# Opening of a three-sub-layer decoder kernel: twelve of its 24 weight units multiplied in fp32 from the landed weights, without high and low parts

## The reference, cut to what matters

```
cond = silu(c)
mod = cond @ ada_w[l] + ada_b[l]                 # 2048 x 18432 weights
sh1, sc1, gt1, sh2, sc2, gt2, sh3, sc3, gt3 = split(mod, 9)
h = rms_norm(x, g_pre) * (1 + sc1) + sh1
gate, up = split(h @ ffn1_w_in, 2)               # 2048 x 11008 weights
y = (silu(gate) * up) @ ffn1_w_out
x = x + 0.5 * gt1 * rms_norm(y, g_post)
... token mixer with sh2, sc2, gt2; second SwiGLU with sh3, sc3, gt3
```

## Time and profile before

| | us |
|---|---|
| median of 3 runs (1950.99 to 1953.15) | 1952.62 |
| the profiled execution's own time | 1952.52 |
| its span, first to last instruction | 1950.7 |
| TensorE busy | 1899.6 (97%) |
| VectorE busy | 1394.3 (71%) |
| ScalarE busy | 846.6 (43%) |
| the opening (to the first group of 8 units) | about 150 |

### The profile page before, as it was taken

The page is one execution under the profiler, slowest core; times in us unless marked ns, Lnnn a source line. Parts: engine busy times, 40 slices in busy tenths (PEclk is TensorE's granted clock), DMA queues, the critical chain, the costliest instruction groups (busy, mean ns, idle before and its releaser), DMA issues.

```text
span 1950.7 us, 21974 instructions
## 1 busy us (share of the span) xinstructions
PE 1899.6 (97%) x8875; PEld 1568.6 (80%) x8875; DVE 1394.3 (71%) x1403; ACT 846.6 (43%) x1075; POOL 79.3 (4%) x137
## 2 busy tenths in 40 slices
PE   5999999999999999899999998999999999999997
PEld 5888888888888889687777786888888888888895
DVE  5979889888888989766775477666665665455565
ACT  4244443444444334564555434644344434443443
POOL 0001000000000000000000010000000000000000
PEclk9999999999999999999999999999999999999999
DMA  9999999999999999564434443766667655556551
GB/s 367 371 354 361 360 339 333 350 346 345 339 342 353 372 322 340 166 191 139 130 110 137 148 151 121 244 239 237 236 230 249 234 194 194 191 186 215 170 199 76
DMA packets 208677, 486.85 MB, mean 250 GB/s; under 512 B 8560, under 2 KB 29760, under 8 KB 193472
## 3 DMA queue, kind: packets, MB, share of 16 engines
q1 hardware_dynamic: 191920, 365.81, 54.3%
q0 software_dynamic: 16224, 117.47, 16.4%
q10 hardware_dynamic: 432, 2.16, 0.3%
HBM read 483.31 MB, written 2.10 MB: 249 GB/s over the span
## 4 chain that ended last, share of the span: by engine, by line
PE 91%; DVE 3%; DMA 2%; ACT 2%; issue 1%; SPq 0%; DVEq 0%; ACTq 0%
PE ps_g L1385 10%; PE ps_u L1385 10%; PE ps_g L1387 10%; PE ps_g L1386 10%; PE ps_u L1387 10%; PE ps_u L1386 10%; PE ps_t L1385 4%; PE ps_t L1387 4%; PE ps_t L1386 4%; PE ps_y L1387 4%; PE ps_y L1385 4%; PE ps_y L1386 4%; DMA ada_raw<-in_ada_w 2%; DVE arena L1131 1%; PE ps_t L1436 1%
## 5 line engine op out<-in xcount | busy, mean ns | idle before, releaser
L882 DVE TENSOR_TENSOR w_lo<-w_raw,w_hi 128x1024 fp32r<-128x1024 f32 (+2 forms) x608 | 724.6, 1200 | 472.6 <-ACT w_hi L544 471.3
L544 ACT ACTIVATE w_hi<-w_raw 128x1024 fp32r<-128x1024 f32 (+2 forms) x608 | 632.9, 1042 | 926.8 <-PE ps_u L1387 331.2
L1385 PE MATMUL ps_g<-w_hi,xT_hi 128*128 128x512 f32 (+1 forms) x880 | 346.1, 393 | 19.2 <-DVE xT_lo L1160 9.1
L1385 PE MATMUL ps_u<-w_hi,xT_hi 128*128 128x512 f32 (+2 forms) x880 | 344.3, 391 | 1.0 <-issue 0.8
L1387 PE MATMUL ps_g<-w_hi,xT_lo 128*128 128x512 f32 (+1 forms) x880 | 340.9, 387 | 0.0
L1386 PE MATMUL ps_g<-w_lo,xT_hi 128*128 128x512 f32 (+1 forms) x880 | 340.6, 387 | 0.0
L1387 PE MATMUL ps_u<-w_hi,xT_lo 128*128 128x512 f32 (+2 forms) x880 | 338.6, 385 | 0.0
L1386 PE MATMUL ps_u<-w_lo,xT_hi 128*128 128x512 f32 (+2 forms) x880 | 338.4, 385 | 0.0
L906 DVE SCALAR_TENSOR_TENSOR arena<-ada_raw,cond,arena 128x2048 f32<-128x2048 f32 x108 | 253.4, 2346 | 5.0 <-DMA ada_raw<-in_ada_w 5.0
L1385 PEld LDWEIGHTS ps_g<-w_hi,xT_hi 128*128 128x128 f32 x880 | 166.1, 189 | 59.2 <-issue 20.4
L1385 PEld LDWEIGHTS ps_u<-w_hi,xT_hi 128*128 128x128 f32 x880 | 165.2, 188 | 36.6 <-issue 6.0
(11 more groups left out here) (246 smaller groups left out, 1717.3 us busy)
## 6 DMA issues: line engine op xcount, KB each, us to landing
w_raw<-in_ffn_w_in SPq DMA_DIRECT2D x157, 1024.0 KB, 6.7
ada_raw<-in_ada_w POOLq DMA_DIRECT2D x112, 1024.0 KB, 6.7
w_raw<-in_ffn_w_out SPq DMA_DIRECT2D x80, 1024.0 KB, 6.7
w_raw<-in_mix_w_in SPq DMA_DIRECT2D x32, 1024.0 KB, 5.1
ada_raw<-in_ada_w SPq DMA_DIRECT2D x32, 512.0 KB, 8.8
arena<-in_ada_w SPq DMA_DIRECT2D x32, 512.0 KB, 9.8
w_raw<-in_mix_w_out SPq DMA_DIRECT2D x16, 1024.0 KB, 5.0
w_raw<-in_ffn_w_in SPq DMA_DIRECT2D x16, 768.0 KB, 5.8
```

The lines of the kernel that those rows point to most:

```text
L544: nc.scalar.activation(w_hi[:, u % 4, 0:n, 0:width], w_raw[:, s, 2 * hf:2 * hf + n, 0:width], ACT.Copy).then_inc(hi_done, 1)
L882: nc.vector.tensor_tensor(w_lo[:, u % 4, 0:n, 0:width], w_raw[:, s, 2 * hf:2 * hf + n, 0:width], w_hi[:, u % 4, 0:n, 0:width].bitcast(F32) ...
L1385: nc.tensor.matmul(o, a_hi[:, k, rows], w_hi[:, b, c, 0:width], start=start, stop=False)
```

## The change

In the three full strips, the units of blocks 0 and 1 (v mod 6 below 4: four of six, twelve in all) are no longer split. TensorE multiplies them in fp32, from the scaled input `xT_raw` and the landed weights `w_raw`: 4 matmuls in the place of 12. The two units of block 2, and all of the short strips, are split as before. What follows from it in the code: the part slots and the counts of `hi_done` and `lo_done` go over the split units alone; ScalarE and VectorE walk a strip's two split units only, with the input pairs and ada tiles set between them; a weight load that takes a raw slot last used by a raw unit waits for TensorE (`pe_used`) in place of VectorE (`lo_done`).

```
+RAW_BLOCKS = 2
+def first_split(v):
+    return v >= 2 * OPENING * FULL or v % (2 * OPENING) // 2 >= RAW_BLOCKS
+SPLIT_UNITS = [v for v in range(8 * OPENING) if first_split(v)]
+SPLIT_SLOT0 = -len(SPLIT_UNITS) % 4
...
 # SP, first_weights
-                need(sp, lo_done, 2 * (q - 4) + 2)
+                before = 2 * (q - 4) + 1
+                if before > 0 and first_split(before):
+                    sp.wait_ge(lo_done, split_count(before))
+                elif before > 0:
+                    sp.wait_ge(pe_used, before + 1)
...
 # ScalarE
-                need(act, pe_used, v - 3)
-                nc.scalar.activation(w_hi[:, v % 4, :, :], w_raw[:, q % 4, 2 * hf:2 * hf + 2, :], ACT.Copy).then_inc(hi_done, 1)
+                if split_count(v) > 4:
+                    act.wait_ge(pe_used, SPLIT_UNITS[split_count(v) - 5] + 1)
+                nc.scalar.activation(w_hi[:, split_slot(v), :, :], w_raw[:, q % 4, 2 * hf:2 * hf + 2, :],
+                                     ACT.Copy).then_inc(hi_done, split_step(v))
             for s in range(STRIPS):
                 start, units = first_units(s)
-                for i in range(units):
-                    first_hi(start + i)
+                split = [v for v in range(start, start + units) if first_split(v)]
+                for i, v in enumerate(split):
+                    first_hi(v)
                     if 2 * i < STRIP_CHUNKS[s][1]:
                         first_xt_hi(STRIP_CHUNKS[s][0] // 2 + i)
...
 # VectorE
-                for i in range(units):
-                    first_lo(start + i)
+                split = [v for v in range(start, start + units) if first_split(v)]
+                early = len(split) // 2
+                for i, v in enumerate(split):
+                    first_lo(v)
...
 # TensorE
+            def raw_unit(v, pair, ps):
+                q, hf = first_place(v)
+                pe.wait_ge(w_landed[q % 4], 16 * (q // 4) + 16)
+                pe.wait_ge(xt_hi_done, pair + 1)
+                for t in range(TILES):
+                    for c in range(2):
+                        k = 2 * pair + c
+                        ins = nc.tensor.matmul(ps[:, t, :], xT_raw[:, k, t * P:(t + 1) * P], w_raw[:, q % 4, 2 * hf + c, :],
+                                               start=k == 0, stop=k == KD - 1)
+                ins.then_inc(pe_used, 1)
```

More of the change, by code:

```diff
@@ L92, in first_place, with split_count, split_slot, split_step @@
     return OPENING * FULL + b, hf
+RAW_BLOCKS = 2
[3 more added lines that the diff above has]
+SPLIT_SLOT0 = -len(SPLIT_UNITS) % 4
+def split_count(v):
+    return SPLIT_UNITS.index(v) + 1
+def split_slot(v):
+    return (SPLIT_UNITS.index(v) + SPLIT_SLOT0) % 4
+def split_step(v):
+    return 1 + 8 * OPENING - len(SPLIT_UNITS) if v == SPLIT_UNITS[-1] else 1
 def ada_total(mod):
@@ L337, in load_group @@
                     dst, src = src_of(s)
-                    sp.wait_ge(lo_done, 8 * g - 8 + 2 * s + 2 + ((0, 2, 1, 0)[s] if g == G_FFN[0] + OPENING else 0))
+                    sp.wait_ge(lo_done, split_count((17, 21, 22, 23)[s]) if g == G_FFN[0] + OPENING else 8 * g - 8 + 2 * s + 2)
                     sp.dma_start(dst, src).then_inc(w_landed[s], 16)
@@ L495, in load_ada @@
                 pool.dma_start(ada_raw[:, a % 2, :], ada_v[k, :, mod * D:(mod + 1) * D]).then_inc(ada_later[a % 2], 16)
-            pool.wait_ge(lo_done, 8 * (G_FFN[0] + OPENING) - 8)
+            pool.wait_ge(lo_done, split_count(17))
             load_ada(0)
@@ L1142, in first_lo @@
                 q, hf = first_place(v)
-                dve.wait_ge(hi_done, v + 1)
-                nc.vector.tensor_tensor(w_lo[:, v % 4, :, :], w_raw[:, q % 4, 2 * hf:2 * hf + 2, :], w_hi[:, v % 4, :, :].bitcast(F32),
-                                        ALU.subtract).then_inc(lo_done, 1)
+                dve.wait_ge(hi_done, split_count(v))
+                nc.vector.tensor_tensor(w_lo[:, split_slot(v), :, :], w_raw[:, q % 4, 2 * hf:2 * hf + 2, :],
+                                        w_hi[:, split_slot(v), :, :].bitcast(F32), ALU.subtract).then_inc(lo_done, split_step(v))
             def first_columns(s):
@@ L1177, in _ @@
                 first_columns(s)
-                for i in range(units):
-                    first_lo(start + i)
+                split = [v for v in range(start, start + units) if first_split(v)]
+                early = len(split) // 2
+                for i, v in enumerate(split):
+                    first_lo(v)
                     if 2 * i < STRIP_CHUNKS[s][1]:
                         first_xt_lo(first_xt + i)
-                    late = i - units // 2 + 1
-                    upto = 2 + (tiles - 2) * late // (units - units // 2) if tiles and late > 0 else done
+                    late = i - early + 1
+                    upto = 2 + (tiles - 2) * late // (len(split) - early) if tiles and late > 0 else done
                     for t in range(done, upto):
@@ L1602, in _ @@
                     pair = STRIP_CHUNKS[s][0] // 2 + hf
-                    pe.wait_ge(lo_done, v + 1)
-                    pe.wait_ge(xt_lo_done, pair + 1)
-                    unit(xT_hi, xT_lo, 2 * pair, v % 4, 2, NB, lambda t: ps[:, t, :], pair == 0, pair == KD // 2 - 1).then_inc(pe_used, 1)
+                    if first_split(v):
+                        pe.wait_ge(lo_done, split_count(v))
+                        pe.wait_ge(xt_lo_done, pair + 1)
+                        unit(xT_hi, xT_lo, 2 * pair, split_slot(v), 2, NB, lambda t: ps[:, t, :], pair == 0, pair == KD // 2 - 1).then_inc(pe_used, 1)
+                    else:
+                        raw_unit(v, pair, ps)
             ffn_pe(0)
```

## The result

The changed kernel takes 1961.01 us (median of 5, 1959.41 to 1964.27) against 1953.15 (5 runs, 1950.99 to 1953.28): ratio 1.0041, 95% interval 1.0031 to 1.0051, or 7.9 us slower. The profiled execution took 1961.01, its span 1959.2 us, against 1952.52 and 1950.7 before: +8.5 us.

What follows compares the result with a forecast made beforehand. TensorE bounds the kernel, with the DMA full from 61.61 to 107.26 us in the opening. Third strip's later start +3.3 and its fp32 units +2.7 give +6.0 on the median 1952.62: 1958.6 us, range 1955.6 to 1961.8.

Steps and rivals of the forecast that it cites:

- The step that failed: Opening's tile loads: with the DMA full, asking earlier changes no landing, so less splitting was costed at nothing.
- Third strip's start: Third full strip begins at 110.6 in place of 107.26 us: +3.3, bounds 109.0 to 112.1.
- the W2 bound: Third strip: W2 lands at 107.4, then 2.7 us on ScalarE, so TensorE starts not before 110.1.
- TensorE's own path: TensorE's work through strips one and two alone would let it start the third strip at 107.7 to 112.1 us.
- the slow clock: First strip's units lose 1.8 us after the wait (0.7 to 2.6); sums and last units slow or at full clock.
- Third strip's five units: Third full strip: four fp32 units at 3.42 in place of 2.74 us, +2.7, with no wait to hide it.
- The pass-count rule: Raw units: 16 passes replace 12, so 3.65 us per unit and 3.6 in the third strip; rejected for the rows.
- Less work for VectorE and ScalarE at nothing: Full strips: twelve copies of 0.95 and twelve subtractions of 1.14 us saved, costed at no gain.
- rival one: Opening: freed VectorE sends tile loads 4.6 us earlier, W2 lands before 101; -1.0, 1951.6 us, chance 0.07.
- The slack of the first two strips: TensorE's gaps between 46 and 107 us, 3.2 us, take part of the fp32 price; nothing after that.
- SP's new waits at nothing: SP queue: W1 and W2 wait for TensorE, delaying the last two ada tiles; costs 0 to 0.6, taken as 0.
- Rival three: Last ada tiles land 3 us later through SP's new wait, strip four's sums wait: +9, 1961.6 us, chance 0.09.

Runs made afterwards that it cites:

- e1: Kernel before, with the twelve units multiplied in fp32 but all units still split and every engine in its old order: 1956.14 us, ratio 1.0017.
- e8: Changed kernel, with half of a full strip's later ada tiles moved ahead of the weight subtractions on VectorE, ScalarE untouched: 1957.44 us, ratio 1.0020.
- e3: Changed kernel, input pairs ahead of high parts on ScalarE; on VectorE input low parts, then half the later tiles, ahead of subtractions: 1955.27 us, ratio 1.0009.
- e5: Changed kernel, same waits and order, but each raw unit is twelve fp32r matmuls that leave out the weights: 1960.45 us, ratio 1.0035.
- e6: Changed kernel, with the last two ada tiles queued ahead of the short strip's W1 and W2 on SP: 1960.36 us, ratio 1.0038.
- e2: Kernel before, no fp32, with ScalarE waiting for W2 at the start of each full strip: 1965.83 us, ratio 1.0067.

## Why the prediction was right, and where its steps failed

The forecast was 1958.6 us, slower; 1961.0 came, inside the range but 0.3 above the forecast's own bounds (to 1960.7). The mechanism is the one it named: the price of the third strip's fp32 units, and a later start of that strip through W2. Two terms were too small, both from one step. That the number fell inside the range is in part luck. In the profiled execution the opening shifted by 9.75 us, beyond the forecast's +4.4 to +8.1; only the medians, at +7.9, lie within it.

Fp32 and order share the loss about evenly in the traces: the fp32 units alone cost 5.1 of 9.75 us (e1), and 5.3 and 5.5 come back when the order is mended and the fp32 stays (e8, e3).

*The step that failed* is "with the DMA full they land one after another at its rate whatever is asked". In these traces the DMA is full only while loads have been issued: 7.7 us without an issue left a slice of 145 GB/s. The forecast had moved ScalarE's first pair behind W2, but had not followed the same delay one engine further, to VectorE's subtractions and the tiles behind them. The first strip's W2 (45.42 against 45.96) and the second's (77.31 against 76.8) landed as forecast; the third's came at 109.64 in place of 107.4 (110.02 in e5, 111.27 in e6). e8 shows the cause: tiles moved ahead on VectorE, nothing else, and W2 is 3.7 us earlier. e2 shows that no fp32 is needed.

*Third strip's start*: forecast +3.3, measured +5.2. From landing to TensorE's start it took 2.84 against 2.7, so all but 0.1 of the excess over the W2 bound is the landing. TensorE's own path without the wait ends at 112.48 - 2.33 = 110.15, inside the 107.7 to 112.1 given. Where in it the slow clock lies was half right: the sums ran at full clock (3.38, as hoped), the last units of strips one and two did not (0.66 and 0.76).

*Third strip's five units*: forecast +2.7, measured +4.5. The price of fp32 held: 0.857 us per matmul against 0.855 from the earlier trace rows, and e5's comparison gives 2.95 for the strip. The 1.8 on top is the slow clock behind the 2.33 us wait. The forecast had this cost in the first strip (1.8 taken, 1.7 measured: 18.12 against 16.4). At the third it had W2's bound up to 2.4 us behind TensorE's own path (110.1 against 107.7) and put the clock behind that wait at nothing.

*The pass-count rule* of the Trainium skill (FP8 and Floating Point Precision, TensorE Precision Notes) would have made the price of the strip 3.6 us. This trace does not agree as to the price: four units at 3.43 in place of 2.74 us are 2.8, and e5's comparison gives 2.95. The row was the better guide. The total of 3.6 + 3.3 would have come nearer to the median, for a wrong reason.

*Less work for VectorE and ScalarE at nothing*: right as to the result here, wrong as a rule. The 13.8 us are real, and rival one's mechanism shows in e8: tiles asked for 5.1 us earlier, W2 landing at 105.90. In the change the order kept it from working. With the order mended (e3, e8) the DMA no longer binds, but then TensorE's path binds at 108.8 to 109.0. Rival one had put that path at 103.6, by taking the sums and last units at full clock and the start at 45.3; in e3 the start was 44.86 and the path still ended 5 us later.

*The slack of the first two strips*: 3.2 us, right as read, and too small for two strips' 5.4: in e1, with the old order, the third strip comes 2.3 late by TensorE's own path. In the change that path is 2.9 late (110.15) and W2 covers it, so that cheap units there (e5) buy nothing.

*SP's new waits at nothing*: right. VectorE took the last tiles at 139.63 and 143.42 with no wait for a DMA, and e6 without the queue's wait is as slow. Rival three is out.

*After 138 us*: the shift was carried to the end less 1.25 us in the profiled pair, of which 1.7 is the clock of one execution at 1150 us; the rest, 0.4 the other way, was not traced. The medians' 7.9 (6.1 to 10.0 by the interval) holds both. What is left open is a finer split than about 2 us: the shift in one execution's opening and the shift of its median differ by up to 2.4 us in the table (e6: 9.7 and 7.3).

## What to carry to other kernels

When an edit makes an in-order engine wait for a later landing, follow the delay through every engine behind it until it reaches a DMA issue: a full DMA stays full only if the engine that frees its buffers isn't waiting for that same DMA. Ask also what binds once the wait is gone: taking it away (e8) gave back about half, because the dearer units stood right behind it. Work taken off an engine buys nothing while its first instruction still waits; put buffer-freeing work ahead of the waiting one. And price a wait ahead of TensorE with the slow clock that follows it: here 2.3 us of waiting cost 1.8 more.

## What the runs showed of the hardware

- A wait of TensorE can be paid twice. At the third strip's start 2.33 us were followed by 8.64 us in which the granted clock was 0.80, for work that takes 6.86 at full clock; 2.47 (e5) and 3.14 us (e2) were each followed by about 1.6 us of loss. After 1.19 (before) and 1.37 us (e6) at the same place the clock was 1.00 and 0.1 us or less was lost. The first units after the opening's first wait of 8.39 us ran at 0.91 over 18.12 us.
- One fp32 matmul of 128x128 by 512 costs 0.857 us, 3.75 times an fp32r one (2.74 us for 12, so 0.228): replacing 12 by 4 is a loss of 25%, not of a third.
- The two profiled executions differ by 1.7 us through the clock in one place: 0.94 against 1.00 over 30 us at 1150 us, in work that is the same in both kernels. Two executions of one and the same program also differ by 1.6 us at the third strip. A single pair of traces can't tell 2 us by a start or an end; a wait or a clock at the place where they arise can.
- A full DMA ran out within 8 us of the last issue here: 7.7 us without an issue gave a slice of 145 GB/s, a gap of 10.3 us (e2, 81.4 to 91.7) slices down to 11.
